# Experts: gated values turned one expert later, inside the next product; low weight parts shared three to three

## The chip, the cores and the metric

The kernel runs on one core of one Trainium2 chip. The metric is the device time of one execution in microseconds. The engines are named as in the profile: PE is TensorE (PEld its weight loads), ACT is ScalarE, DVE is VectorE, POOL is GpSimd, SP is SyncE, which here issues the weight loads. All matrices are float32; a product is made of three passes over a high and a low part (fp32r).

## The reference, cut to what matters

Two transformer blocks over 512 tokens of width 1024. The change lies in the last stage, a mixture of 16 experts in 4 groups of 4, each 1024 to 256 to 1024. Every token picks one group, and two experts in it:

```python
g_sel = argmax(hf @ w_r1 + b_r1)                 # one of 4 groups
top_p, top_i = top_k(softmax(e_logits[g_sel]), 2)   # two of its 4 experts
combine = one_hot(expert_id) * (g_w * top_p)     # zero for all other experts
hid = silu(hf @ w_gate[e]) * (hf @ w_up[e])      # 512 x 256 for each expert e
out = sum_e (combine[:, e] * hid) @ w_down[e]
x = x + out
```

## The kernel before, in words

**Order.** `make_order()` writes out one list of steps, and every engine runs through it in that order with its own part of each step. Semaphores of `Progress` (`X.after(key)` to wait, `X.done(key)` to signal) tie the engines together. Each engine works its own steps strictly one after the other.

**Sorted tokens.** `route 0` (DVE) finds the group of each token, `sort` its place in group order, `resort` (PE, ACT, DVE) turns the normalised tokens into `mix_hi`, `mix_lo`, sorted by group. The 512 sorted tokens are four blocks s of 128. A flag for each group and block says whether any token of the block is in the group. Visit v = 4e + s is expert e on block s. In this run's data 28 of the 64 visits are active: blocks 0 and 1 for experts 0 to 3, 1 and 2 for experts 4 to 7, 2 and 3 for 8 to 11, block 3 for 12 to 15. PE and DVE branch on the flag and do one tiny operation for a skipped visit (`skip`), which signals all of the visit's keys at once. ACT has no branch: it does its two activations for skipped visits too. `route 1` computes `combine`, and `combine_s` sorts it with PE.

**A visit, before.** On PE: 24 matmuls `ps[s] += mix * w` over 8 chunks k (left half of the 512 columns is gate, right half up); then `down(v - 4)`, the 12 matmuls of the same block's previous expert (not for the first expert of a group); then it waits for `hid` of this visit and transposes its two halves into bank 4. On ACT: `e_silu` = silu of the gate half after the up product, then `hid_hi` = rounded copy of the transposed values. On DVE: `hid` = up half times `e_silu`, then `hid_lo` = transposed values minus `hid_hi`, then `add(v - 4)`: two operations that add the down product, scaled by `combine_s`, to `y_exp`. `finish(v)` is the down product and `add` of a group's last expert; it stands ahead of the first visit of the next group on the same block. `hid` and `e_silu` have two slots, used in turn.

**Weights.** Each expert has six units of 128x1024: units 0 to 3 are gate and up (two chunks of k each), 4 and 5 are down. SP loads unit g into one of four slots `raw` once the low part of unit g - 4 is done. ACT makes the high part (line 1406), POOL (line 744) or DVE (line 2409) the low part `raw` minus high; `low_by(g)` says who: before, POOL for units 0 to 3, DVE for 4 and 5. Split parts lie in twelve slots, two experts deep: `w_hi`/`w_lo` and the first of `more_hi`/`more_lo` for even experts, the rest of `more`, `far_hi`/`far_lo`, `gap_w` and `end_w` for odd ones; a slot is free when PE is through with the expert two before. The steps `("weights", n)` in the order say up to which unit ACT, POOL and DVE split: at the end of expert e's visits units 4 and 5 of expert e + 1; ahead of visit (e + 1, 0) units 0, 1, 2 of expert e + 2; ahead of visit (e + 1, 1) unit 3 of expert e + 2. So between two experts ACT's queue holds the high parts of units 4, 5, 0, 1, 2, with unit 3 one visit later.

**Banks.** The up product of block s uses PSUM bank s, the transposes bank 4, down banks 5 and 6; `claim` waits for the last readers of a bank.

## Time and profile before

| | |
|---|---|
| time of three runs | 1829.16, 1830.31, 1831.88 us; median 1830.31 |
| profiled execution, its own time | 1819.03 us |
| its span, first to last instruction | 1817.2 us |
| mean granted clock of PE | 0.912 |
| PE busy | 1554.0 us, 86% |
| ACT, DVE, POOL busy | 686.0 (38%), 646.7 (36%), 565.4 us (31%) |
| memory traffic | 142.09 MB, mean 78 GB/s |
| expert stage, first visit to last down | 1455 to 1790 us |

The granted clock is the share of full speed that PE was given: 1.0 is 2.4 GHz, 0.5 is 1.2 GHz. Times in the timelines are counted from the span's start. A duration of a matmul in the profile overlaps the next one; the distance of two starts is what a matmul costs.

### The profile page before, as it was taken

What the parts mean: (1) busy time and instruction counts of PE and PEld (TensorE: products, weight loads), DVE (VectorE), ACT (ScalarE), POOL (GpSimd) and SP (SyncE); (2) the same over time, 40 slices, a digit from 0 to 9 for tenths busy, and PEclk for the clock granted to TensorE, in tenths of its full rate; (3) what the DMA queues carried; (4) which work ended last, traced back from release to release, by engine and by line L of the source; (5) the groups of instructions that cost most, each with busy time, mean ns of one, the idle gap of its engine ahead of it and who ended that gap; (6) DMA issues with size and microseconds to landing.
All of it is one profiled execution on the core that took longest, in us unless ns stands there. A gap on an engine that the chain in (4) does not pass through costs nothing. (4 is left out here: it accounts for less than half of the span.)

```text
span 1817.2 us, 18907 instructions
## 1 busy us (share of the span) xinstructions
PE 1554.0 (86%) x7008; PEld 1195.6 (66%) x7008; DVE 646.7 (36%) x1377; ACT 686.0 (38%) x1166; POOL 565.4 (31%) x253
## 2 busy tenths in 40 slices
PE   4998999989798899899557899989997688888877
PEld 3776666667576677767445687767875466666655
DVE  2276343233102322138844223043222443232333
ACT  4542224122445543243245424444232344343452
POOL 2264210003242233324200346522441444444460
PEclk9999998579899899999869999989998789998988
DMA  4222101002221122212100224411221144444451
GB/s 127 70 82 58 47 25 36 14 12 78 64 79 61 47 87 76 81 47 93 47 1 1 96 99 129 128 47 53 98 72 54 47 128 151 140 140 140 140 187 47
DMA packets 96000, 142.09 MB, mean 78 GB/s; under 512 B 11649, under 2 KB 46648, under 8 KB 95896
## 3 DMA queue, kind: packets, MB, share of 16 engines
q1 hardware_dynamic: 92948, 136.21, 23.4%
q10 hardware_dynamic: 2660, 4.45, 0.7%
q8 instruction: 69, 1.13, 0.3%
q14 instruction: 35, 0.29, 0.1%
q0 software_dynamic: 288, 0.02, 0.0%
HBM read 138.55 MB, written 2.10 MB: 77 GB/s over the span
## 5 line engine op out<-in xcount | busy, mean ns | idle before, releaser
L744 POOL TENSOR_TENSOR w_lo<-raw,w_hi 128x1024 fp32r<-128x1024 f32 (+1 forms) x191 | 455.7, 2404 | 1069.1 <-ACT w_hi L1406 1069.0
L1406 ACT ACTIVATE w_hi<-raw 128x1024 fp32r<-128x1024 f32 (+1 forms) x191 | 191.5, 1033 | 267.2 <-PE ps L796 241.6
L794 PE MATMUL ps<-w_hi,act_hi 128*128 128x512 f32 (+1 forms) x560 | 226.8, 405 | 17.9 <-ACT dq L1543 7.2
L795 PE MATMUL ps<-w_lo,act_hi 128*128 128x512 f32 (+1 forms) x560 | 222.0, 396 | 0.0
L796 PE MATMUL ps<-w_hi,act_lo 128*128 128x512 f32 (+1 forms) x560 | 221.5, 396 | 0.0
L794 PE MATMUL ps<-w_hi,mix_hi 128*128 128x512 f32 x432 | 174.1, 403 | 11.2 <-DVE mix_lo L1935 10.2
L795 PE MATMUL ps<-w_lo,mix_hi 128*128 128x512 f32 x432 | 172.1, 398 | 0.0
L796 PE MATMUL ps<-w_hi,mix_lo 128*128 128x512 f32 x432 | 171.9, 398 | 0.0
L794 PEld LDWEIGHTS ps<-w_hi,act_hi 128*128 128x128 f32 (+1 forms) x560 | 106.0, 189 | 49.1 <-POOL w_lo L744 8.3
L796 PEld LDWEIGHTS ps<-w_hi,act_lo 128*128 128x128 f32 (+1 forms) x560 | 105.8, 189 | 26.0
L794 PE MATMUL ps<-act_hi,w_hi 128*128 128x512 f32 (+5 forms) x288 | 110.0, 384 | 14.5 <-POOL w_lo L744 9.9
L795 PEld LDWEIGHTS ps<-w_lo,act_hi 128*128 128x128 f32 (+1 forms) x560 | 106.1, 189 | 23.1 <-issue 0.3
L795 PE MATMUL ps<-act_lo,w_hi 128*128 128x512 f32 (+5 forms) x288 | 109.9, 384 | 0.0
L796 PE MATMUL ps<-act_hi,w_lo 128*128 128x512 f32 (+5 forms) x288 | 108.4, 380 | 0.0
L794 PEld LDWEIGHTS ps<-w_hi,mix_hi 128*128 128x128 f32 x432 | 83.7, 194 | 31.2 <-DVE mix_lo L1935 9.4
L796 PEld LDWEIGHTS ps<-w_hi,mix_lo 128*128 128x128 f32 x432 | 83.5, 193 | 18.0
L795 PEld LDWEIGHTS ps<-w_lo,mix_hi 128*128 128x128 f32 x432 | 83.6, 193 | 17.2
L794 PEld LDWEIGHTS ps<-act_hi,w_hi 128*128 128x128 f32 (+3 forms) x288 | 53.7, 187 | 29.3 <-issue 6.4
L744 POOL TENSOR_TENSOR more_lo<-raw,more_hi 128x1024 fp32r<-128x1024 f32 x16 | 41.2, 2590 | 91.7 <-ACT more_hi L1406 91.7
L796 PEld LDWEIGHTS ps<-act_hi,w_lo 128*128 128x128 f32 (+3 forms) x288 | 53.9, 188 | 13.6 <-issue 2.1
L795 PEld LDWEIGHTS ps<-act_lo,w_hi 128*128 128x128 f32 (+3 forms) x288 | 53.6, 186 | 13.1 <-issue 1.6
L2386 DVE TENSOR_TENSOR hid<-ps,e_silu 128x256 f32<-128x256 f32 x28 | 11.9, 424 | 138.2 <-ACT e_silu L1575 138.2
(452 smaller groups left out, 2643.7 us busy)
## 6 DMA issues: line engine op xcount, KB each, us to landing
raw<-in_w_in SPq DMA_DIRECT2D x92, 512.0 KB, 3.4
raw<-in_w_gate SPq DMA_DIRECT2D x64, 256.0 KB, 3.0
raw<-in_w_up SPq DMA_DIRECT2D x64, 256.0 KB, 3.8
raw<-in_w_down SPq DMA_DIRECT2D x32, 512.0 KB, 4.5
raw<-in_w_out SPq DMA_DIRECT2D x16, 512.0 KB, 3.5
raw<-in_w_mem_kv SPq DMA_DIRECT2D x16, 512.0 KB, 3.8
raw<-in_w_o_gla SPq DMA_DIRECT2D x8, 512.0 KB, 3.4
raw<-in_w_o_dsa SPq DMA_DIRECT2D x8, 512.0 KB, 3.4
```

The lines of the kernel that those rows point to most:

```text
L744: pool.tensor_tensor(lo[:, 0:a], raw[:, g % RAW_SLOTS, 0:a], hi[:, 0:a].bitcast(F32), ALU.subtract).then_inc(*POOL.done(("w_lo", g)))
L794: pe.matmul(dst, l_hi, r_hi, start=start, stop=False, skip_group_check=skip)
L795: pe.matmul(dst, l_hi, r_lo, start=False, stop=False, skip_group_check=skip)
L796: return pe.matmul(dst, l_lo, r_hi, start=False, stop=stop, skip_group_check=skip)
L1406: nc.scalar.activation(split_slot(g)[0][:, 0:a], raw[:, g % RAW_SLOTS, 0:a], ACTF.Copy).then_inc(*ACT.done(("w_hi", g)))
L2386: dve.tensor_tensor(hid[:, v % 2, :], ps[:, s, D_EXP:2 * D_EXP], e_silu[:, v % 2, :], ALU.mult).then_inc(*DVE.done(("hid", v)))
```

## The change

- `hid` of visit v is no longer transposed at the end of visit v. The new `turn(v)` does it inside the up product of visit v + 4 (same block, next expert), ahead of chunk 4; ACT's `hid_high(v)` and DVE's `hid_low(v)` follow there. For the last expert of a group, `finish(v)` does turn, high and low parts and down.
- `finish` stands behind the visit of the same block instead of ahead of it.
- `hid` has one slot for each block (four), `e_silu` has one in all.
- `low_by`: POOL makes the low parts of units 0 to 2, DVE of 3 to 5. PE waits for unit 2's low part ahead of chunk 0 and for unit 3's ahead of chunk 6.
- `route 1` stands behind visit 3 instead of visit 0, next to `combine_s`.

```diff
--- before.py
+++ after.py
@@ -280,15 +280,13 @@
 
 
     for v in range(NT * N_EXP):
-        if v >= NT and v // NT % 4 == 0:
-            order += [("finish", v - NT)]
         if v % NT < 2:
             order += [("weights", E_UNITS * (v // NT + 1) + 3 + v % NT)]
         order += [("visit", v)]
-        if v == 0:
-            order += [("route", 1)]
+        if v >= NT and v // NT % 4 == 0:
+            order += [("finish", v - NT)]
         if v == NT - 1:
-            order += [("combine_s",)]
+            order += [("route", 1), ("combine_s",)]
         if v % NT == NT - 1:
             order += [("weights", E_UNITS * (v // NT + 2))]
     order += [("finish", NT * (N_EXP - 1) + s) for s in range(NT)]
@@ -468,8 +466,8 @@
         combine_s = sb("combine_s", [P, NT, N_EXP], SC + 59)
         so = sb("so", [P, 8, 16], SC + 59.25)
         flags = sb("flags", [P, 16], SC + 59.75, mybir.dt.int32)
-        hid = sb("hid", [P, 2, D_EXP], SC + 60)
-        e_silu = sb("e_silu", [P, 2, D_EXP], SC + 62)
+        hid = sb("hid", [P, NT, D_EXP], SC + 60)
+        e_silu = sb("e_silu", [P, D_EXP], SC + 56)
         skipped = sb("skipped", [1, 2, NT * N_EXP], SC + 72)
         iota = sb("iota", [P, SEQ], SC + 48)
         before_t = sb("before_t", [P, P], SC + 50)
@@ -594,7 +592,7 @@
 
         def low_by(g):
 
-            return DVE if g >= expert_unit and (g - expert_unit) % E_UNITS >= 4 else POOL
+            return DVE if g >= expert_unit and (g - expert_unit) % E_UNITS >= 3 else POOL
 
         def slot_free(g):
 
@@ -1238,6 +1236,15 @@
                 mm.then_inc(*done)
                 return done
 
+            def turn(v):
+
+                s = v % NT
+                pe.wait_ge(*DVE.after("hid", v))
+                claim(4, (ACT, ("hid_hi", v)), (DVE, ("hid_lo", v)))
+                for c in range(2):
+                    tr = pe.transpose(ps[:, 4, P * c:P * c + P], hid[:, s, P * c:P * c + P], ident[:, :])
+                tr.then_inc(*PE.done(("turn", v)))
+
             def visit(v):
 
 
@@ -1245,29 +1252,29 @@
                 g0 = expert_unit + E_UNITS * e
                 bank = s
                 with pe.If_ne(flag(v), 0):
-                    pe.wait_ge(*POOL.after("w_lo", g0 + 3))
                     claim(bank, (ACT, ("e_silu", v)), (DVE, ("hid", v)))
                     for k in range(KC):
+                        if k == 4 and e % 4:
+                            turn(v - NT)
+                        if k in (0, 6):
+                            low = g0 + (2 if k == 0 else 3)
+                            pe.wait_ge(*low_by(low).after("w_lo", low))
                         wh, wl = [x[:, 512 * (k % 2):512 * (k % 2) + 512] for x in split_slot(g0 + k // 2)]
                         rows = slice(P * s, P * s + P)
                         mm = product(ps[:, bank, :], mix_hi[:, k, rows], mix_lo[:, k, rows], wh, wl, k == 0, k == KC - 1)
-                    mm.then_inc(*PE.done(("up", v), *([("unit", g0 + i) for i in range(4)] if s == NT - 1 else [])))
+                    done = PE.done(("up", v), *([("unit", g0 + i) for i in range(4)] if s == NT - 1 else []))
+                    mm.then_inc(*done)
                     if e % 4:
-                        down(v - NT)
-                    pe.wait_ge(*DVE.after("hid", v))
-                    claim(4, (ACT, ("hid_hi", v)), (DVE, ("hid_lo", v)))
-                    for c in range(2):
-                        tr = pe.transpose(ps[:, 4, P * c:P * c + P], hid[:, v % 2, P * c:P * c + P], ident[:, :])
-                    done = PE.done(("turn", v))
-                    tr.then_inc(*done)
+                        done = down(v - NT)
                 with pe.Else():
-                    skip(done, 3 if e % 4 else 2)
+                    skip(done, 3 if e % 4 else 1)
 
             def finish(v):
                 with pe.If_ne(flag(v), 0):
+                    turn(v)
                     done = down(v)
                 with pe.Else():
-                    skip(done, 1)
+                    skip(done, 2)
 
             def unsort():
 
@@ -1566,20 +1573,28 @@
                     nc.scalar.activation(mix_hi[:, k, :], ps[:, k % 4, :], ACTF.Copy,
                                          scale=col("g_ffn_2", k)).then_inc(*ACT.done(("s_hi", k)))
 
-            def visit(v):
-
-                act.wait_ge(*PE.after("up", v))
-                if v >= 2:
-                    act.wait_ge(*ACT.after("e_silu", v - 2))
-                    act.wait_ge(*DVE.after("hid", v - 2))
-                nc.scalar.activation(e_silu[:, v % 2, :], ps[:, v % NT, 0:D_EXP], ACTF.Silu).then_inc(*ACT.done(("e_silu", v)))
+            last_turned = [None]
+
+            def hid_high(v):
+
                 act.wait_ge(*PE.after("turn", v))
-                if v:
-                    act.wait_ge(*DVE.after("hid_lo", v - 1))
+                if last_turned[0] is not None:
+                    act.wait_ge(*DVE.after("hid_lo", last_turned[0]))
                 if v >= NT:
                     act.wait_ge(*ACT.after("hid_hi", v - NT))
                     act.wait_ge(*PE.after("down", v - NT))
+                last_turned[0] = v
                 nc.scalar.activation(hid_hi[:, v % NT, :], ps[:, 4, 0:D_EXP], ACTF.Copy).then_inc(*ACT.done(("hid_hi", v)))
+
+            def visit(v):
+
+                if v // NT % 4:
+                    hid_high(v - NT)
+                act.wait_ge(*PE.after("up", v))
+                if v:
+                    act.wait_ge(*ACT.after("e_silu", v - 1))
+                    act.wait_ge(*DVE.after("hid", v - 1))
+                nc.scalar.activation(e_silu[:, :], ps[:, v % NT, 0:D_EXP], ACTF.Silu).then_inc(*ACT.done(("e_silu", v)))
 
             def unsort():
                 for s in range(NT):
@@ -1828,7 +1843,7 @@
                      "idx_scores": idx_scores, "dsa_prepare": dsa_prepare, "dsa_scale": dsa_scale, "dsa_scores": dsa_scores,
                      "dsa_turn": dsa_turn, "dsa_values": dsa_values, "mem_prepare": mem_prepare, "mem_scale": mem_scale,
                      "mem_scores": mem_scores, "mem_turn": mem_turn, "mem_values": mem_values, "route": route,
-                     "visit": visit, "unsort": unsort}
+                     "visit": visit, "finish": hid_high, "unsort": unsort}
             act.wait_ge(zeroed, 2)
             load_gains(act, 1)
             for step, *a in order:
@@ -2380,25 +2395,30 @@
             def visit(v):
                 e, s = divmod(v, NT)
                 with dve.If_ne(flag(v), 0):
+                    if e % 4:
+                        hid_low(v - NT)
                     dve.wait_ge(*ACT.after("e_silu", v))
-                    if v >= 2:
-                        dve.wait_ge(*PE.after("turn", v - 2))
-                    dve.tensor_tensor(hid[:, v % 2, :], ps[:, s, D_EXP:2 * D_EXP], e_silu[:, v % 2, :],
-                                      ALU.mult).then_inc(*DVE.done(("hid", v)))
-                    dve.wait_ge(*ACT.after("hid_hi", v))
-                    done = DVE.done(("hid_lo", v))
-                    dve.scalar_tensor_tensor(hid_lo[:, s, :], ps[:, 4, 0:D_EXP], 1.0, hid_hi[:, s, :].bitcast(F32),
-                                             ALU.mult, ALU.subtract).then_inc(*done)
+                    if v >= NT:
+                        dve.wait_ge(*PE.after("turn", v - NT))
+                    done = DVE.done(("hid", v))
+                    dve.tensor_tensor(hid[:, s, :], ps[:, s, D_EXP:2 * D_EXP], e_silu[:, :], ALU.mult).then_inc(*done)
                     if e % 4:
                         done = add(v - NT)
                 with dve.Else():
-                    skip(0, v, done, 3 if e % 4 else 2)
+                    skip(0, v, done, 3 if e % 4 else 1)
+
+            def hid_low(v):
+
+                dve.wait_ge(*ACT.after("hid_hi", v))
+                dve.scalar_tensor_tensor(hid_lo[:, v % NT, :], ps[:, 4, 0:D_EXP], 1.0, hid_hi[:, v % NT, :].bitcast(F32),
+                                         ALU.mult, ALU.subtract).then_inc(*DVE.done(("hid_lo", v)))
 
             def finish(v):
                 with dve.If_ne(flag(v), 0):
+                    hid_low(v)
                     done = add(v)
                 with dve.Else():
-                    skip(1, v, done, 1)
+                    skip(1, v, done, 2)
 
             def split_low(upto):
```

## Rows read from the trace of the kernel before

**Rows 1.** Busy time by stretch: expert stage; busy PE, PEld, DVE, ACT, POOL, clock, DMA.

```profile
1455.00:1790.00 335.00, 282.48 (x1194) 220.47 (x1194) 112.30 (x217) 135.30 (x226) 146.94 (x60) 0.91 0.44 139
```

**Rows 2.** Waits of PE from 1455 to 1792: total us, times, longest.

```profile
PE ps L1260 <- DVE hid L2386: 28.4, 15, 5.3
PE ps L794 <- DVE skipped L2366: 19.3, 7, 4.8
```

**Rows 3.** Timeline of PE, experts 2 and 3: start, length, what, wait before.

```profile
1503.53 0.50 PE L794 MATMUL ps<-w_hi,mix_hi 128*128 128x512 f32 x1
...
1513.60 0.44 PE L1260 MATMUL ps<-ident,hid 128*128 128x128 f32 x2 [1.60 <-DVE hid L2386]
1514.07 0.47 PE L794 MATMUL ps<-w_hi,mix_hi 128*128 128x512 f32 x1
...
1522.36 0.38 PE L1260 MATMUL ps<-ident,hid 128*128 128x128 f32 x2
...
1522.84 0.50 PE L794 MATMUL ps<-more_hi,mix_hi 128*128 128x512 f32 x1
```

**Rows 4.** Timeline of ACT and DVE in expert 2.

```profile
1506.04 3.90 ACT L1406 ACTIVATE more_hi<-raw 128x1024 fp32r<-128x1024 f32 x4
1507.12 2.36 DVE L2409 TENSOR_TENSOR more_lo<-raw,more_hi 128x1024 fp32r<-128x1024 f32 x2 [1.39 <-ACT more_hi L1406]
...
1511.76 1.06 ACT L1406 ACTIVATE far_hi<-raw 128x1024 fp32r<-128x1024 f32 x1 [1.83 <-DMA raw<-in_w_up]
...
1512.72 0.36 ACT L1575 ACTIVATE e_silu<-ps 128x256 f32<-128x256 f32 x1
```

**Rows 5.** Timeline in expert 10.

```profile
1681.16 0.24 PE L1222 MATMUL ps<-ones 128*1 128x1 f32 x4
...
1683.34 2.35 DVE L2409 TENSOR_TENSOR more_lo<-raw,more_hi 128x1024 fp32r<-128x1024 f32 x2
...
1688.11 1.06 ACT L1406 ACTIVATE far_hi<-raw 128x1024 fp32r<-128x1024 f32 x1 [2.67 <-DMA raw<-in_w_up]
...
1690.21 1.06 ACT L1406 ACTIVATE far_hi<-raw 128x1024 fp32r<-128x1024 f32 x1 [0.49 <-DMA raw<-in_w_up]
...
1692.60 0.44 PE L1260 MATMUL ps<-ident,hid 128*128 128x128 f32 x2 [2.82 <-DVE hid L2386]
```

**Rows 6.** Timeline where DVE and POOL work at once.

```profile
1472.89 2.34 POOL L744 TENSOR_TENSOR far_lo<-raw,far_hi 128x1024 fp32r<-128x1024 f32 x1 [8.52 <-ACT far_hi L1406]
1472.92 2.34 DVE L2307 TENSOR_TENSOR rt<-rt 128x16 f32<-128x16 f32 x1
...
1706.80 3.37 POOL L744 TENSOR_TENSOR w_lo<-raw,w_hi 128x1024 fp32r<-128x1024 f32 x1 [11.87 <-ACT w_hi L1406]
```

**Rows 7.** Timeline of PE: starts and ends of the groups of experts.

```profile
1541.74 0.38 PE L1260 MATMUL ps<-ident,hid 128*128 128x128 f32 x2
...
1569.60 0.47 PE L794 MATMUL ps<-more_hi,mix_hi 128*128 128x512 f32 x1
...
1631.64 0.38 PE L1260 MATMUL ps<-ident,hid 128*128 128x128 f32 x2
...
1661.95 0.47 PE L794 MATMUL ps<-more_hi,mix_hi 128*128 128x512 f32 x1
...
1724.02 0.38 PE L1260 MATMUL ps<-ident,hid 128*128 128x128 f32 x2
...
1771.93 0.79 PE L794 MATMUL ps<-more_hi,mix_hi 128*128 128x512 f32 x1 [0.65 <-POOL far_lo L744]
...
1784.71 0.47 PE L794 MATMUL ps<-gap_w,hid_hi 128*128 128x512 f32 x1 [2.40 <-DVE skipped L2366]
```

**Rows 8.** Timeline of DVE in the sort.

```profile
1429.57 2.25 DVE L2333 TENSOR_TENSOR so<-so 128x16 f32<-128x16 f32 x1
```

**Rows 9.** Busy time by stretch, behind two waits; columns as in rows 1.

```profile
1637.00:1642.20 5.20, 5.19 (x12) 3.82 (x12) 0.00 (x0) 2.75 (x5) 5.20 (x3) 0.52 0.90 283
1693.30:1697.30 4.00, 4.00 (x11) 3.20 (x12) 1.74 (x3) 0.15 (x1) 1.63 (x1) 0.59 0.74 233
```

## The prediction, made before the change ran

> **What bounds the kernel now.** I read the page first, then the busy time and clock of stretches, then what PE waited for, and last the timelines of single experts. The change touches the expert stage and a few steps ahead of it: 335 of 1817.2 us, in which PE is busy 282.5 us at a mean granted clock of 0.91 [rows 1]. So PE is the bound, and what can be had is its idle time and its time at 1.2 GHz. Its waits fall in two groups [rows 2]: 28.4 us ahead of the two transposes of `hid` (line 1260), and 19.3 us ahead of the down product (the "skipped" named there stands behind `add` on DVE, which frees banks 5 and 6); the latter come where the token group changes.
>
> Call T the start of the first active block's up product of an expert. From 1514.07 to 1522.36, 36 matmuls take 8.29 us: 0.230 each, so 5.5 for the up product and 2.8 for down [rows 3]. In expert 2, T is 1503.53 and the transposes start at T+10.1, having waited 1.6 [rows 3]. Why: `e_silu` stands on ACT behind the high parts of weight units 4, 5, 0, 1 and 2 (I call them the burst). ACT starts it at T+2.5; unit 2 can load only when DVE has done the low part of unit 4 (end T+4.8, half of the pair's 2.36), and ACT takes it up at T+8.2, 3.4 us later; ACT is free 0.96 after that, and from the start of `e_silu` to PE's start it is 0.88 (ACT's 0.36, the rest DVE's `hid` and latencies) [rows 3, 4]. In expert 10 the first active block is the third: T is 1681.4, behind the skips, unit 3 stands ahead of `e_silu` too and starts at T+8.8, and PE waits 2.8 us [rows 5]. The reader is to see that ACT's queue, not ACT's work, makes PE wait.
>
> **The change part by part.**
> *The transposes move into the next expert's up product.* The old values are long there, so PE's wait on `hid` goes. But `hid_hi` of the old block is now the first thing ACT does in a visit, behind the same burst, and PE needs it, and `hid_lo` after it, for the down product at T+5.5+0.44 = T+5.95 (0.44: the two transposes [rows 3]), where the transposes were due at T+8.3. The deadline comes 2.3 us earlier; the burst starts earlier only by the transposes and the `hid_hi` that left its front. Late next: `hid_lo`, with it down, then `add`.
>
> *Experts 2, 3 (blocks 0 and 1 active).* ACT still waits for DVE's skip behind `add`: burst at T+2.1 instead of T+2.5. Unit 2 is off ACT at 2.1+5.7+0.96 = T+8.7; `hid_hi` and `hid_lo` have the 128x256 shapes of `e_silu` and `hid`, so by the same 0.88 PE goes at T+9.55. PE stands 3.6 us. The expert lasts 9.55+2.75+8.7 (second visit with its transposes)+0.25 (skips) = 21.3, against 1522.84-1503.53 = 19.3 [rows 3]: for two experts **+4.1**.
>
> *Low part of unit 3 on DVE.* Where the first active block is not block 0, DVE meets it ahead of `hid_lo`. It lasts 1.2 us (two together 2.35 [rows 5]). And DVE and GpSimd do not run two-input work from SBUF side by side: a 128x16 sum on DVE lasted 2.34 us beside a GpSimd low part that started with it, and a GpSimd part that met a DVE one lasted 3.37 instead of 2.34 [rows 6]. For experts 5 to 7 I get, from T: burst 0.3, DVE's unit 4 done 2.6, unit 2 off ACT 7.05, block 0's empty pair 7.6, unit 3 taken up 2.6+1.1+4.5 = 8.2 (4.5 as in [rows 5]) and done 9.3. GpSimd has unit 0 from 3.3 and its three parts, one lengthened by DVE (2.7+2.34+2.34), last until 10.7; so DVE's unit 3 ends 11.9 and, with `hid_lo` close behind (0.4, the smaller half of the 0.88), PE goes at 12.3. Bound below: no holding, 11.0. I take the held one, since [rows 6] are these shapes. The expert is 12.3+2.75+8.7+0.35 = 24.1, three less the last skips 71.9, against 1631.64-1569.60 = 62.0 [rows 7]: **+9.9**. In experts 9 to 11 block 1's skip on DVE stands behind unit 3 and holds ACT's next `hid_hi` as well: burst -0.2, GpSimd until 10.65, DVE 11.8, skip 11.95, 0.88: PE goes at 12.9. Expert 24.65, three 73.7 against 1724.02-1661.95 = 62.1: **+11.6** [rows 7]. Experts 13 and 14 (one active block): GpSimd until 10.1, DVE 11.3, two empty ACT steps, PE at 12.9, expert 12.9+2.75+0.75 = 16.4.
>
> The Trainium skill (GPSIMD Engine Reference, Performance versus the Vector engine) puts elementwise work on VectorE at about twice GpSimd's speed. By that ratio alone the moved part costs the chain nothing: PE would go at about T+10.2 instead of 12.3 and 12.9 in eight experts, and the sum would be 20 us lower than mine. The ratio agrees with [rows 5, 6], 1.2 against 2.34; what the rows add is the place in DVE's queue.
>
> *Finish behind visit, at the three group changes.* The up product of the new group can cover the old group's DVE work. But down now needs `hid_hi`, which stands behind the whole burst: after group 0 (block 0's visit is skipped, so nothing covers it) the burst starts 2.25 us after the last down, unit 2 is off ACT at 8.9, an empty `e_silu` 0.3, 0.88: down starts at 10.1, a wait of some 9 us. Then down 2.75, up 5.5, one uncovered pair with the transposes 1.55, down 2.75, up 5.5, skips 0.5: 28.65 against 1569.60-1541.74 = 27.9 [rows 7]: **+0.8**. After group 1, unit 3 in front as above, down starts at 12.7: 31.2 against 1661.95-1631.64 = 30.3: **+0.9**; a wait of 4.8 [rows 2] makes room for one of 11. After group 2: 26.35, and with 2x16.4 for experts 13 and 14 it is 59.15 against 1771.93-1724.02 = 47.9: **+11.3** [rows 7].
>
> *The end.* Behind expert 15 no units 0 to 3 follow, so no stall: 8.7, and the last down starts 2.05 later (DVE's `add`, then `hid_lo`): 10.75 against 1784.71-1771.93 = 12.8 [rows 7]: **-2.0**.
>
> *Ahead of the experts.* GpSimd has three low parts instead of four beside the sort, so a DVE sum of 128x16, held for 2.25 us [rows 8], runs free: -2.1 on the path to the sorted tokens. Unit 3's low part on DVE then lies between sort and resort, hidden by PE's first resort products. `route 1` moves from visit 0 to visit 3 and starts 3.5 us later, behind visit 1's `hid`; its held sum [rows 6] goes (-2.2), and so do the waits of two transposes. Together **-1.9**, between -2.1 and +2.2.
>
> `e_silu` in one slot and `hid` in four cost nothing: each `e_silu` waits for a `hid` that was done while PE ran the product in between; without that cover, 0.4 a visit. PE's wait for unit 3 at chunk 6: nothing, that part is done an expert earlier.
>
> Sum at full clock: 4.1+9.9+11.6+0.8+0.9+11.3-2.0-1.9 = **+34.7**.
>
> *The clock.* In the 5.2 us behind a wait of 4.8, PE did the twelve matmuls of a down at a granted 0.52, that is at 1.2 GHz: 2.4 us lost; behind the 2.8 us wait of expert 10, 4 us at 0.59, 1.6 lost [rows 9]; behind the 1.6 us of expert 2 nothing [rows 3]. The lengths of before used above hold such losses, mine hold none. I add 1.7 for each of experts 2 and 3, and 2.0 (between 1.6 and 2.4) for each of eight longer stalls and three group changes: 3.4+22 = **+25**.
>
> Total +60. The profiled execution took 1819.0 us (span 1817.2, 1.8 around it); the median of the runs shown is 1830.3, 11 above, with nothing in the trace to say where. The sum is put on the median: 1890.
>
> **The rivals.**
> *Faster: the values are ready when down needs them.* Both waits of [rows 2] go (47.7), seven uncovered pairs in the finishes cost 1.0 each, the clock gives back half of the 0.09x335 = 30 us of [rows 1], and start and end help by 4: 1830-48+7-15-4 = 1770. It decides where ACT can take up unit 2 by T+4.0 in experts 2 and 3; the steps above say T+7.8. For it: PE's own waits are just those that the move removes. Against it: the burst's chain runs over three engines and a load, and the change shortens none. 8%.
> *Stalls as forecast, prices short.* GpSimd does not hold DVE in the burst (-13.6), and the clock costs between nothing and the 25: +21 to +46, 1851 to 1876. For it: the wait of 1.6 us brought no slow clock [rows 3]. 22%.
> *No change:* the burst starts so much earlier that it pays for the earlier deadline, 3 us an expert more than above. 3%.
> *Worse:* unit 2 lands 4.5 us behind the low part, as unit 3 does [rows 5], and each stall costs 2.4: +12+4, 1906 and above. 5%.
> The forecast, 1876 to 1906, has 62%.
>
> **How the numbers follow.** 1890 is the likeliest case. The range takes in short prices and forecast up to 1904: 1851 to 1904. Slower by over 0.2% (3.7 us, about what a measurement of this kernel can tell from no change): 62+22+5 = 89%; within it 3%; faster 8%.
>
> **What would show it.** PE's largest idle groups would be the first matmul of down (line 794, `gap_w` or `more_hi` with `hid_hi`) behind DVE's `hid_lo`: ten of 3.5 to 7 us and three of 9 to 11 or a little more; the waits of the transposes would be near zero. ACT's `hid_hi` of the first active block would start right behind unit 2 (or 3). GpSimd would have 45 low parts in the stage. Wrong if down follows the up product without a gap; half wrong if the gaps are 2 us shorter, or if DVE's unit 3 lasts 1.2 us each time; the clock part is wrong if the stretches behind the gaps show 1.0.

## The result, and the profile after

The changed kernel took 1889.47 us (median of four runs, 1887.75 to 1897.11). The kernel before took 1829.74 us (four runs, 1828.4 to 1831.88). The ratio is 1.0333, with a 95% interval of 1.0302 to 1.0365: 59.7 us slower. The prediction had said 1890 us, and had given 89% to slower.

The profiled execution took 1891.06 us (span 1889.2), against 1819.03 for the profiled one before. That is 72.0 us, 12 more than the medians are apart. The profiled execution before lay 11 us under its median, as the prediction said; what made it so fast I have not found. All lengths below are of this pair of profiles.

This is the busy time of the expert stage after, from the first up product to the end of the last down product. Its columns are those of [rows 1].

```profile
1457.40:1861.80 404.40, 284.94 (x1189) 224.28 (x1190) 138.03 (x231) 136.16 (x224) 109.59 (x45) 0.84 0.36 115
```

PE does the same work (282.5 us in [rows 1], 284.9 now), in 404 us instead of 335. The clock falls from 0.91 to 0.84. GpSimd has 45 low parts instead of 60.

What PE waited for, from 1455 to 1864 (total us, times, longest), to be held against [rows 2]:

```profile
PE ps L1245 <- ACT hid_hi L1587: 45.7, 9, 9.0
PE ps L1245 <- DVE skipped L2381: 37.9, 4, 11.6
PE ps L792 <- DVE hid_lo L2413: 24.4, 9, 7.5
PE ps L1196 <- DVE combine L2324: 10.4, 1, 10.4
```

Before, 47.7 us stood ahead of transposes and down products. Now it is 108.0 us, and most of it (83.6) stands ahead of the transposes (line 1245), which were to be free. Only 24.4 us stand where the prediction looked for all of it.

Expert 3 is of the kind that the forecast had right. The timeline of all engines, to be read with [rows 3, 4]:

```profile
1528.66 0.50 PE L792 MATMUL ps<-more_hi,mix_hi 128*128 128x512 f32 x1
...
1530.68 1.06 ACT L1413 ACTIVATE gap_w<-raw 128x1024 fp32r<-128x1024 f32 x1
1531.51 0.38 PE L1245 MATMUL ps<-ident,hid 128*128 128x128 f32 x2
...
1536.65 1.06 ACT L1413 ACTIVATE w_hi<-raw 128x1024 fp32r<-128x1024 f32 x1 [2.07 <-DMA raw<-in_w_up]
1537.61 0.37 ACT L1587 ACTIVATE hid_hi<-ps 128x256 fp32r<-128x256 f32 x1
...
1538.01 0.42 DVE L2413 SCALAR_TENSOR_TENSOR hid_lo<-ps,hid_hi 128x256 fp32r<-128x256 f32 x1 [3.87 <-ACT hid_hi L1587]
...
1538.54 0.47 PE L792 MATMUL ps<-more_hi,hid_hi 128*128 128x512 f32 x1 [3.90 <-DVE hid_lo L2413]
```

T, the start of the expert's first active up product, is 1528.66. The transposes run in mid-product, at T+2.9, without a wait. `hid_hi` could follow at once. But ACT is in its burst, and unit 2 lands late: ACT takes it up at T+8.0 and only then does `hid_hi`. PE starts down at T+9.9 after 3.90 us. The forecast was T+9.55 and 3.6.

Expert 10 is of the kind that the forecast had wrong. The same view, to be read with [rows 5]:

```profile
1716.05 0.50 PE L792 MATMUL ps<-w_hi,mix_hi 128*128 128x512 f32 x1
...
1717.31 2.35 DVE L2429 TENSOR_TENSOR more_lo<-raw,more_hi 128x1024 fp32r<-128x1024 f32 x2
...
1722.01 1.06 ACT L1413 ACTIVATE far_hi<-raw 128x1024 fp32r<-128x1024 f32 x1 [2.06 <-DMA raw<-in_w_up]
1722.97 0.37 ACT L1587 ACTIVATE hid_hi<-ps 128x256 fp32r<-128x256 f32 x1
...
1724.13 2.34 POOL L742 TENSOR_TENSOR far_lo<-raw,far_hi 128x1024 fp32r<-128x1024 f32 x1
1724.50 1.06 ACT L1413 ACTIVATE far_hi<-raw 128x1024 fp32r<-128x1024 f32 x1 [0.89 <-DMA raw<-in_w_up]
...
1725.59 1.97 DVE L2429 TENSOR_TENSOR far_lo<-raw,far_hi 128x1024 fp32r<-128x1024 f32 x1 [5.88 <-ACT far_hi L1413]
...
1727.48 0.13 DVE L2381 TENSOR_SCALAR skipped<-ones 1x1 f32<-1x1 f32 x1
1727.76 0.66 PE L1245 MATMUL ps<-ident,hid 128*128 128x128 f32 x2 [8.70 <-DVE skipped L2381]
```

Here blocks 0 and 1 are skipped and blocks 2 and 3 active. PE stops at T+3.0, in the middle of its up product, and stands 8.70 us. `turn(v)` calls `claim(4, ...)`: it may write bank 4 only when the readers of the turn before it have counted. That turn is the one of skipped block 1. Its reader on DVE is the skip at 1727.48, and this stands behind unit 3's low part, which stands behind unit 3's high part on ACT. So the transposes of an active block wait for a block that does nothing. The low part itself lasts 1.97 us instead of 1.22; GpSimd's began at 1724.13 and ended 1.09 us before it (more of this in the last section).

The groups' starts and ends after, to be held against [rows 7] (PE; the skips stand where a group's last expert ends):

```profile
1551.46 0.29 PE L1220 MATMUL ps<-ones 128*1 128x1 f32 x6
...
1582.33 0.50 PE L792 MATMUL ps<-more_hi,mix_hi 128*128 128x512 f32 x1
...
1654.81 0.34 PE L1220 MATMUL ps<-ones 128*1 128x1 f32 x8
...
1688.24 0.50 PE L792 MATMUL ps<-more_hi,mix_hi 128*128 128x512 f32 x1
...
1772.29 0.36 PE L1220 MATMUL ps<-ones 128*1 128x1 f32 x9
...
1784.24 0.66 PE L1245 MATMUL ps<-ident,hid 128*128 128x128 f32 x2 [11.56 <-DVE skipped L2381]
...
1842.99 0.50 PE L792 MATMUL ps<-more_hi,mix_hi 128*128 128x512 f32 x1
...
1857.35 0.76 PE L792 MATMUL ps<-gap_w,hid_hi 128*128 128x512 f32 x1 [0.98 <-DVE hid_lo L2413]
```

From these and [rows 7], in us:

| part | before | after | measured | forecast, clock included |
|---|---|---|---|---|
| experts 2 and 3 | 38.2 | 45.7 | +7.5 | +7.5 |
| change from group 0 to 1 | 27.9 | 30.9 | +3.0 | +2.8 |
| experts 5 to 7 | 62.0 | 72.5 | +10.4 | +15.9 |
| change from group 1 to 2 | 30.3 | 33.4 | +3.1 | +2.9 |
| experts 9 to 11 | 62.1 | 84.1 | +22.0 | +17.6 |
| change from 2 to 3, experts 13, 14 | 47.9 | 70.7 | +22.8 | +17.3 |
| expert 15 to the last down | 12.8 | 14.4 | +1.6 | -2.0 |
| norm and sort, to expert 2 | | | -1.2 | -1.9 |
| ahead of the experts, and behind them | | | +2.9 | 0 |
| sum | | | +72.1 | +60.1 |

The held sum of [rows 8] runs free, as forecast (DVE in the sort, after):

```profile
1433.05 0.18 DVE L2348 TENSOR_TENSOR so<-so 128x16 f32<-128x16 f32 x1
```

The stretches behind three waits and one without a wait in front, columns as in [rows 9]:

```profile
1538.50:1543.10 4.60, 4.56 (x13) 3.65 (x14) 0.27 (x1) 1.06 (x1) 2.50 (x2) 0.63 0.71 246
1727.70:1735.00 7.30, 7.24 (x27) 6.00 (x28) 0.85 (x2) 0.77 (x2) 0.00 (x0) 0.80 0.45 144
1784.20:1791.40 7.20, 6.18 (x15) 4.68 (x16) 0.45 (x2) 0.72 (x2) 0.00 (x0) 0.50 0.43 143
1595.60:1601.30 5.70, 5.70 (x26) 4.67 (x27) 1.83 (x3) 0.38 (x1) 0.00 (x0) 1.00 0.53 176
```

Behind 3.90 us of waiting the clock is 0.63, behind 11.56 us it is 0.50, which is 1.2 GHz; in the 7.3 us behind the 8.70 us of expert 10 it is 0.80. Twelve matmuls of a down then take up to 5.3 us instead of 2.8 (start to start: 1785.88 to 1791.13, against 1769.48 to 1772.29).

### The profile page after: what moved, and what is told of

It is laid out like the page before. It is cut to its first block and busy times, and to the rows that moved or that the text cites. A ratio compares the mean times of both kernels' runs of the same rounds, so it can differ in the third digit from the quotient of the medians.

```text
span 1889.2 us, 18908 instructions
## 1 busy us (share of the span) xinstructions
PE 1560.0 (83%) x7008; PEld 1201.8 (64%) x7008; DVE 672.5 (36%) x1393; ACT 687.4 (36%) x1166; POOL 525.3 (28%) x237
## 3 DMA queue, kind: packets, MB, share of 16 engines
q10 hardware_dynamic: 2660, 4.45, 0.8%
## 5 line engine op out<-in xcount | busy, mean ns | idle before, releaser
L742 POOL TENSOR_TENSOR w_lo<-raw,w_hi 128x1024 fp32r<-128x1024 f32 (+1 forms) x183 | 435.4, 2397 | 1123.8 <-ACT w_hi L1413 1123.8
L792 PE MATMUL ps<-w_hi,act_hi 128*128 128x512 f32 (+1 forms) x560 | 227.8, 407 | 19.5 <-POOL w_lo L742 8.1
L1245 PE MATMUL ps<-ident,hid 128*128 128x128 f32 x56 | 13.8, 336 | 83.6 <-ACT hid_hi L1587 45.7
L2390 DVE SCALAR_TENSOR_TENSOR y_exp<-ps,combine_s,y_exp 128x512 f32<-128x512 f32 x56 | 39.5, 746 | 76.2 <-PE ps L794 76.2
L1597 ACT ACTIVATE e_silu<-ps 128x256 f32<-128x256 f32 x64 | 24.3, 380 | 111.4 <-PE ps L794 109.0
```

Source lines behind the costliest of these rows:

```text
L742: pool.tensor_tensor(lo[:, 0:a], raw[:, g % RAW_SLOTS, 0:a], hi[:, 0:a].bitcast(F32), ALU.subtract).then_inc(*POOL.done(("w_lo", g)))
L792: pe.matmul(dst, l_hi, r_hi, start=start, stop=False, skip_group_check=skip)
L1245: tr = pe.transpose(ps[:, 4, P * c:P * c + P], hid[:, s, P * c:P * c + P], ident[:, :])
L1597: nc.scalar.activation(e_silu[:, :], ps[:, v % NT, 0:D_EXP], ACTF.Silu).then_inc(*ACT.done(("e_silu", v)))
L2390: op = dve.scalar_tensor_tensor(y, ps[:, 5 + n, :], combine_s[:, s, e:e + 1], y, ALU.mult, ALU.add)
```

## The experiments

Each kernel is timed against the kernel before on the same chip. The stage is the time in the profiled execution from the start of the first up product to the start of the last down product. It leaves out what varies ahead of the experts (last section), so parts are compared by it. But each stage length comes from a single execution: what it says of the difference to the kernel before and what the medians say lie 0.2 to 10.7 us apart in the rows below. A stage difference of a few us is therefore a hint and no proof. Medians decide on faster or slower.

| run | built on | ratio to before (95%) | median us | stage us |
|---|---|---|---|---|
| kernel before | | 1 | 1826.0 to 1829.7 | 329.5 |
| changed kernel | | 1.0333 (1.0302 to 1.0365) | 1889.47 | 399.9 |
| two banks | changed | 1.0313 (1.0278 to 1.0349) | 1887.16 | 391.1 |
| unit 3 on GpSimd | changed | 1.0286 (1.0242 to 1.0331) | 1879.46 | 383.3 |
| finish first | changed | 1.0328 (1.0285 to 1.037) | 1886.15 | 396.2 |
| split behind | changed | 1.0233 (1.0203 to 1.0262) | 1869.44 | 369.2 |
| unit 3 on VectorE | before | 1.0135 (1.0097 to 1.0173) | 1852.65 | 364.6 |
| delay alone | before | 1.0272 (1.0231 to 1.0313) | 1878.41 | 378.1 |
| spread, with delay | changed | 1.0089 (1.0056 to 1.0121) | 1843.31 | 345.2 |
| spread, no delay | before | 1.003 (0.9998 to 1.0061) | 1832.46 | 341.6 |
| spread 2, with delay | changed | 1.0073 (1.0047 to 1.0098) | 1837.78 | 343.0 |
| spread 2, unit 2 on VectorE | changed | 1.0097 (1.007 to 1.0125) | 1842.29 | 347.9 |
| spread 2, no delay | before | 0.9981 (0.9961 to 1.0) | 1822.05 | 321.8 |
| mixed order, no delay | before | 0.9981 (0.9962 to 1.0001) | 1823.68 | 325.5 |

### Two banks for the delayed transposes

```diff
-                claim(4, (ACT, ("hid_hi", v)), (DVE, ("hid_lo", v)))
+                claim(7 if v % 2 else 4, (ACT, ("hid_hi", v)), (DVE, ("hid_lo", v)))
```

The two transposes and their readers take the same bank. PE's skip, which wrote bank 7, now writes the bank that its step stands for, and waits for that bank's readers first; PE stood 1.5 us at such a skip, once.

> The changed kernel with one edit: the delayed transposes of even blocks go to bank 4 of PSUM, those of odd blocks to bank 7. Theory: in the groups whose first block is a skipped one before the active ones, TensorE stands at the transposes (8.93, 8.70 and 8.71 us in experts 9 to 11, 11.56 at the change from group 2 to group 3) because it may not write bank 4 before ScalarE and VectorE have read what the block before left there, although that block was skipped. With a second bank the transposes go ahead of the four last chunks, those four (about 4.2 us) then run beside the split, and the down product waits for what is left. Each of the five waits of experts 9 to 11, 13 and 14 that fall on the transposes, and the change 2 to 3, ends 3 to 4 us earlier: 12 to 20 us less than the changed kernel in all, 1870 to 1878 us; TensorE's idle time ahead of its transposes falls from 83.6 us to under 60. Rival: what is late is VectorE's own share (unit 3's low part, then the low part of the gated values), which stands behind the split whatever the bank: the down product then waits for as long as the transposes did, and the time is 1887 to 1892 us.

PE's waits in this run, from 1468 to 1863:

```profile
PE ps L792 <- DVE hid_lo L2420: 54.6, 12, 10.5
PE ps L1250 <- DVE skipped L2388: 20.8, 5, 8.6
PE ps L1250 <- ACT hid_hi L1594: 20.7, 4, 7.4
```

The wait at the transposes halves, from 83.6 to 41.5 us, but most of it comes back at the down product, where 24.4 us become 54.6. Expert 10 takes 23.8 us instead of 27.4, as the theory said, and expert 11 with the change to group 3 loses 6.9 together. But experts 13 and 14 keep 20 us each: their active block 3 needs bank 7, and the block that held it last is the skipped block 1, whose skip stands behind unit 3's low part. Experts 5 to 7 become dearer (25.3 to 27.3 us each, from 23.7 to 24.8). There the transposes now come early, the four chunks behind them run while ACT is still in its burst, and PE then stands 6.5 to 7.2 us at the down product. The stage loses 8.9 us of the 12 to 20 expected. By medians the gain can't be told from nothing, and the time, 1887.16 us, is the rival's. So the bank is shown as a cause of where PE waits, and of 3.6 us in expert 10; as a price of the whole, 9 us of stage are a hint. The rest is the queue behind it.

### Unit 3's low part back on GpSimd

```diff
-            return DVE if g >= expert_unit and (g - expert_unit) % E_UNITS >= 3 else POOL
+            return DVE if g >= expert_unit and (g - expert_unit) % E_UNITS >= 4 else POOL
```

> The changed kernel with one edit: the low part of the experts' unit 3 goes back from VectorE to GpSimd, as in the kernel before. Theory (VectorE's share stands ahead of the values that TensorE waits for): in experts 9 to 11, 13 and 14 the wait at the transposes loses what VectorE spends on that part, 1.97 us plus what it waits for a collision with GpSimd's, so about 2 us each, and as much at the two changes behind group 1: 10 to 14 us less than the changed kernel, 1875 to 1880 us. Experts 2, 3 and 5 to 7 stay within 1 us of 22.9 and 24.0. Rival (the wait is set by the units' high parts on ScalarE or by their transfers; VectorE's part lies in its shadow): no change, 1887 to 1892 us.

1879.46 us: inside the expected range. The wait of expert 9 falls from 8.93 to 6.67 us. What PE waits for ahead of the transposes is now always ACT (from 1463 to 1851):

```profile
PE ps L1245 <- ACT hid_hi L1587: 72.7, 13, 9.9
PE ps L792 <- DVE hid_lo L2413: 22.5, 9, 7.6
```

### Finish first

```diff
+        if v >= NT and v // NT % 4 == 0:
+            order += [("finish", v - NT)]
         if v % NT < 2:
             order += [("weights", E_UNITS * (v // NT + 1) + 3 + v % NT)]
         order += [("visit", v)]
-        if v >= NT and v // NT % 4 == 0:
-            order += [("finish", v - NT)]
```

> The changed kernel with one edit in the written order: at the change from one group of experts to the next, the finish of a block stands ahead of the split of the units and of the visit again, as in the kernel before. Theory (behind the visit, the finish's high and low part stand behind unit 2's or unit 3's split on ScalarE and VectorE): the stalls of 9.34, 11.61 and 11.56 us at the three changes shrink by 3 to 6 us each, 9 to 18 us less than the changed kernel, 1872 to 1881 us. Rival (the product of the visit covers the finish's chain of transposes, high part and low part; with the finish first nothing does): each active block's chain of about 2.1 us lies bare three times, and the time is 1889 to 1896 us.

The theory fell short: the stage loses 3.7 us and the median 3.3, not 9 to 18, and the intervals of this and the changed kernel overlap almost wholly. The change from group 0 to 1 gets 3.0 us shorter (27.8 instead of 30.9), the second stays as it was (33.5), the third loses 1.6. With the finish first, `hid_hi` stands ahead of unit 2 (PE waits 3.5 us instead of 7.5 for the first down), but then the chain from the up product to the next down lies bare, as the rival said. The two nearly cancel; the rival's 1889 to 1896 us did not come either.

### Split behind the visit

```diff
-        if v % NT < 2:
-            order += [("weights", E_UNITS * (v // NT + 1) + 3 + v % NT)]
         order += [("visit", v)]
...
+        if v % NT < 2:
+            order += [("weights", E_UNITS * (v // NT + 1) + 3 + v % NT)]
```

> The changed kernel with one edit in the written order: the split of the next expert's units 2 and 3 is queued behind the visit of block 0 and 1 and no longer ahead of it. Theory (each stall is the block's high and low part queued behind a split whose unit comes late): the 3.8 and 3.9 us waits of experts 2 and 3 and some 1.7 us at the experts before them go (about 9 us), those of experts 5 to 7 lose about 4 us each (12 us), experts 9 to 11 lose the wait on the skipped block but keep the split of unit 3 ahead of their own block (3 us each, 9 us), experts 13 and 14 keep theirs. 20 to 30 us less than the changed kernel, 1859 to 1870 us. Rival (the weights are what is late: the slots come free and the units land too late, and the split is needed where it stands): the next expert's first product waits for units 2 and 3 instead, by about as much as was saved, and the time is 1883 to 1895 us.

The stage lasts 369.2 us, 30.7 less than in the changed kernel; the time is 1869.44 us, inside the expected range. This is the clearest proof of the queue. Expert 3, all engines:

```profile
1533.66 1.06 ACT L1413 ACTIVATE gap_w<-raw 128x1024 fp32r<-128x1024 f32 x1
1534.61 1.06 ACT L1413 ACTIVATE end_w<-raw 128x1024 fp32r<-128x1024 f32 x1
...
1535.56 0.38 ACT L1587 ACTIVATE hid_hi<-ps 128x256 fp32r<-128x256 f32 x1
...
1537.07 2.00 ACT L1413 ACTIVATE w_hi<-raw 128x1024 fp32r<-128x1024 f32 x2
...
1537.55 0.47 PE L792 MATMUL ps<-more_hi,hid_hi 128*128 128x512 f32 x1 [0.80 <-DVE hid_lo L2413]
```

Only units 4 and 5 stand in front of `hid_hi`, and the late unit 2 stands behind it. The wait falls from 3.90 to 0.80 us, and expert 2 from 22.9 to 18.6. Expert 6 falls from 23.9 to 19.9 and expert 10 from 27.4 to 23.6, though there units split behind a skipped block still stand in front. Experts 13 and 14 stay at 19.0 and 20.3.

### Unit 3's low part on VectorE, alone

```diff
-            return DVE if g >= expert_unit and (g - expert_unit) % E_UNITS >= 4 else POOL
+            return DVE if g >= expert_unit and (g - expert_unit) % E_UNITS >= 3 else POOL
```

PE waits for units 0 to 2 at the first chunk and for unit 3 at the seventh, as in the changed kernel.

> The kernel before with one part of the change alone: the low part of the experts' unit 3 is VectorE's and no longer GpSimd's (TensorE waits for units 0 to 2 at the first chunk and for unit 3 at the seventh). Theory (VectorE's share stands ahead of the gated product in its queue, and GpSimd and VectorE hold each other): in experts 9 to 11, 13 and 14 the wait at the transposes grows by 1.2 to 2 us each, as much at two group changes, less 2 at the sort: 5 to 12 us more than the kernel before, 1835 to 1842 us. Rival (nothing stands behind VectorE's part while the values are turned in the same expert): within 3 us of the kernel before, 1827 to 1833 us.

1852.65 us, against 1826.04: 26.6 us, more than twice what the theory allowed and far from its rival. PE's waits ahead of the transposes are 28.1 us, as before (28.4); what grew is the wait ahead of down, from 19.3 us to this (from 1453 to 1822):

```profile
PE ps L794 <- DVE skipped L2368: 50.4, 11, 6.9
```

Expert 9, DVE, GpSimd and PE:

```profile
1675.74 2.33 POOL L744 TENSOR_TENSOR w_lo<-raw,w_hi 128x1024 fp32r<-128x1024 f32 x1
...
1676.43 2.73 DVE L2411 TENSOR_TENSOR w_lo<-raw,w_hi 128x1024 fp32r<-128x1024 f32 x1 [5.21 <-ACT w_hi L1408]
...
1679.08 0.13 DVE L2368 TENSOR_SCALAR skipped<-ones 1x1 f32<-1x1 f32 x1
...
1679.47 0.76 PE L794 MATMUL ps<-more_hi,hid_hi 128*128 128x512 f32 x1 [3.94 <-DVE skipped L2368]
```

I had looked only at the product `hid` behind this low part. The skip of block 1 stands behind it too. It is also the "reader" of banks 5 and 6, so PE's next down product waits for it: 3.94 us here, 6.88 and 6.87 in experts 10 and 11, where the kernel before did not wait at down. It is the same trap as the one at bank 4.

### The delay alone

The changed kernel with unit 3 on GpSimd, with the finish first and with `("route", 1)` behind visit 0.

> The changed kernel with unit 3's low part on GpSimd, the finish ahead of the split and of the visit, and the second half of the routing behind visit 0, all three as in the kernel before: what is left is the delay of the transposes by one expert, with the one slot for the activated values. Theory (the delay is the main price and the parts add up): the stage from the first up product to the last down product lasted 399.9 us in the changed kernel and 329.5 before; going back to GpSimd took 16.7 us of it and the finish 3.7, so some 380 us are left and the time is 1872 to 1880 us. Rival (the parts multiply: without VectorE's share in front the delayed values come in time for down): the stage lasts under 355 us, and the time is under 1856 us.

1878.41 us, stage 378.1: as expected. The delay with its slots costs 52 us by itself. Alone the delay and the low part on VectorE cost 52 and 27 us; together, in the changed kernel, with the finish and the place of `route 1` as well, they cost 60. My reading is that both lengthen the same wait; it was not tested further.

### The splits spread over the visits

```diff
         order += [("visit", v)]
...
+        if v % NT < 2:
+            order += [("weights", E_UNITS * (v // NT + 1) + 1 + v % NT)]
         if v % NT == NT - 1:
             order += [("weights", E_UNITS * (v // NT + 2))]
```

The two steps ahead of the visits are gone, and PE waits for each unit at its own two chunks. First with the delay and the two banks:

> The changed kernel with the two banks of the earlier run and the splits spread over the visits, each behind the visit of its block: unit 0 of the next expert behind block 0, unit 1 behind block 1, units 2 to 5 behind block 3; TensorE waits for each unit at its own two chunks. Theory (nothing but the split that stands ahead of the delayed values costs time): experts 2 and 3 take 18.6 us, 5 to 7 about 19.5, 9 to 11 about 20, 13 and 14 about 12, the group changes lose 5 us each; the stage takes 320 to 335 us and the time is 1808 to 1830 us, at or below the kernel before. Rival (units 0 and 1 of the next expert are loaded only when units 2 and 3 have been split, so TensorE now waits for weights at the start of each expert or each unit): 2 to 4 us for each of 12 experts, 1835 to 1870 us.

And in the kernel before, with unit 3's low part on VectorE:

> The kernel before with the same spread of the splits, unit 3's low part on VectorE and TensorE's waits unit by unit; the transposes stay in their own expert. Theory A (the waits of 1.6 to 3.3 us at the transposes in the kernel before have the same cause, a late unit's split ahead of the activation): they shrink to the bare 0.9 us, the stage loses 10 to 20 us, 1810 to 1820 us, as low as the same spread with the delay. Theory B (only the delay needs the early deadline, and the kernel before is bound otherwise): 1826 to 1836 us, and the version with the delay is lower by 10 us or more.

With the delay: 1843.31 us and a stage of 345.2, so 55 us of the stage come back by order and banks together. It is still 0.9% above the kernel before, above the 1830 that I expected and inside the rival's range. Without the delay: 1832.46 us, 1.0030 with an interval that reaches to 1. Theory B's numbers for this kernel hold, but its other half does not: the version with the delay is 11 us slower by the medians (their stages are 3.7 us apart), not faster. With the delay, PE now waits 2.1 us for GpSimd's low part of unit 2 in experts 2 and 3, as the rival said, and 7.2 and 7.8 us at the group changes.

### Units 4 and 5 later, products in place

```diff
         if v % NT == NT - 1:
-            order += [("weights", E_UNITS * (v // NT + 2))]
+            order += [("weights", E_UNITS * (v // NT + 1) + 4)]
...
-                nc.scalar.activation(e_silu[:, :], ps[:, v % NT, 0:D_EXP], ACTF.Silu)
+                nc.scalar.activation(hid[:, v % NT, :], ps[:, v % NT, 0:D_EXP], ACTF.Silu)
```

> The spread version with the delay, with two further edits: units 4 and 5 of an expert are split behind its own block 0 (and behind the finish there) and no longer at the end of the expert before, so only units 2 and 3 are split between two experts; and the activated values are written to the block's own slot of the gated values and multiplied in place, so ScalarE no longer waits for VectorE's product of the block before. Theory (what is left of the price is split work ahead of the delayed values at the group changes, 7.2, 7.8 and 8.1 us of waiting, and the split's late start in the others): the changes lose 3 to 5 us each, experts 2, 3, 5 to 7 some 1.5 us each, the stage goes from 345 to 320 to 328 us and the time to 1815 to 1828 us. Rival (the splits are only moved from one place ahead of the values to another): the waits come back at block 0 of each expert, 1838 us or more.

Then with unit 2's low part on VectorE and unit 3's on GpSimd:

> The same with one more edit: unit 2's low part is VectorE's and unit 3's GpSimd's, so that TensorE's fifth chunk no longer waits for GpSimd (2.1 us in experts 2 and 3, 1 to 1.8 us in experts 5 to 7 of the spread version). Theory: 1 to 1.5 us less for each of five experts, 5 to 8 us less than without the edit, 1808 to 1822 us. Rival (VectorE's part now stands ahead of its additions and the low parts of the values): nothing, or up to 5 us more.

And both edits of order and engines in the kernel before, transposes in their own expert:

> The kernel before, transposes in their own expert, with the same order of splits and the same engines for the low parts as the run with unit 2 on VectorE. Theory A (with the split out of the way the delay saves TensorE the bare 0.9 us of every block, some 24 blocks): this version is 10 to 20 us slower than that one. Theory B (the delay saves nothing because hid's high and low parts come late all the same): equal within 4 us or faster.

The first is 1837.78 us, a miss: 15 to 28 us were expected and 5.5 came, and the stage lost 2.2 us instead of 17 to 25. The second is 1842.29 us: the rival holds, moving the low part gains nothing (4.5 us more). The third is 1822.05 us, 20 us less than its twin with the delay. Theory A had it 10 to 20 us more; theory B, equal or faster, holds.

The order of splits and the engines of the low parts are the same in the last two, the twins. They are not equal in all else: the one with the delay also has the two banks, the product in place, the finish behind the visit and `route 1` behind visit 3. So the 20 us are not the delay's alone by the medians. Their stages are 26.0 us apart, and 23.6 of these lie inside the experts, where neither finish nor `route 1` stands. With the delay experts 5 to 7 are 4.1 us longer, 9 to 11 12.5, 13 and 14 6.3 and 15 3.4, but experts 2 and 3 are 2.5 us shorter (37.7 against 40.3); the three group changes together are 0.8 longer, the stretch ahead of expert 2 1.6. In this order of splits the delay costs where skipped blocks stand ahead of the first active one, and not where block 0 is active. The two banks and the product in place, which came with it, were not tested apart from it. Expert 10 of the second run, with the delay (all engines), and then of the third, without it (PE), show why:

```profile
1683.37 0.50 PE L791 MATMUL ps<-w_hi,mix_hi 128*128 128x512 f32 x1
...
1689.87 1.06 ACT L1419 ACTIVATE more_hi<-raw 128x1024 fp32r<-128x1024 f32 x1 [3.89 <-DMA raw<-in_w_up]
...
1692.17 1.06 ACT L1419 ACTIVATE more_hi<-raw 128x1024 fp32r<-128x1024 f32 x1 [0.70 <-DMA raw<-in_w_up]
1693.14 0.37 ACT L1593 ACTIVATE hid_hi<-ps 128x256 fp32r<-128x256 f32 x1
...
1694.30 0.59 PE L791 MATMUL ps<-gap_w,hid_hi 128*128 128x512 f32 x1 [4.51 <-DVE hid L2409]
```

```profile
1691.31 0.47 PE L794 MATMUL ps<-gap_w,hid_hi 128*128 128x512 f32 x1 [0.83 <-DVE skipped L2368]
...
1694.22 0.44 PE L1262 MATMUL ps<-ident,hid 128*128 128x128 f32 x2
```

The expert starts at 1683.37 there and at 1683.30 here. With the delay, PE is through with its up product at T+6.4 and wants `hid_lo`; but `hid_hi` stands behind units 2 and 3, which ACT takes up as they land, at T+6.5 and T+8.8, and down starts at T+10.9. Without the delay, down starts at T+8.0 after 0.83 us, and ACT's next work for PE is wanted only at the transposes behind down, at T+10.9, where PE does not wait for it. The expert takes 23.9 us with the delay and 20.2 without.

### The mixed order

> The kernel before, transposes in their own expert, with the spread order of the run before it only behind the visits of experts 4 to 10, where that run's experts were shorter (5 to 7 and 9 to 11: 18.8 to 20.2 us, against 19.3 to 22.2 in the kernel before); behind the other visits the order of the kernel before, since experts 1 to 3 had become 1 us longer each (TensorE waits 2.1 us for unit 2's low part) and the change from group 2 to 3 3.4 us longer (7.8 us of waiting instead of 4.6). Unit 2's low part is VectorE's where the order is the spread one, otherwise all as in the kernel before. Theory (the parts add up): the gain of the run before it, 4.6 us, and these 5 to 6 us on top: 1814 to 1820 us, 0.4 to 0.7% under the kernel before. Rival (what one expert gains, the next loses, since units arrive in one order through four slots): 1821 to 1827 us.

1823.68 us: the rival holds. Experts 2 and 3, which had become longer, are no longer so (19.5 and 19.4 us), but expert 11, the first behind the spread order, now waits 4.45 us at its transposes. What one place gains, the next gives back. Both versions without the delay lie 0.2% under the kernel before, with intervals that end at 1. I take neither for a proven gain.

## Why the prediction was right, and where it was right for the wrong reason

- **The bound.** "ACT's queue, not ACT's work, makes PE wait" held, and taking late units out from in front of `hid_hi` gave back 31 us of stage (split behind), or 55 together with the two banks (spread).
- **The earlier deadline.** The step "The deadline comes 2.3 us earlier" is the best reading of what remained when the order of splits and the engines were equal: 20 us between the medians of the twins, with the differences that are named there. It did not cost in experts 2 and 3, where the twin with the delay is 2.5 us shorter.
- **Experts 2 and 3.** Wait 3.8 and 3.9 us (3.6 forecast), and the down behind it took 1.6 us longer (4.4 instead of 2.8), where the clock term had 1.7. The sum is exact.
- **Group changes 0 to 1 and 1 to 2.** +3.0 and +3.1, forecast +2.8 and +2.9. The places of the waits differ (7.8 us stood at the transposes at the second change), the lengths do not.
- **Experts 5 to 7: too dear by 5.5 us.** The down started at T+12.4 in expert 6 (forecast 12.3). But PE had waited at the transposes, and the slow clock behind that wait fell on the four chunks that ran while DVE finished (4.25 us instead of 2.8, and the down behind them 2.8). The 2.0 us of clock that the forecast added for each did not come on top.
- **Experts 9 to 11, 13 and 14, and the third change: too cheap by 10 us.** The step that failed is "The old values are long there, so PE's wait on `hid` goes", taken to mean that the transposes need not wait at all. The forecast had the skip of block 1 on DVE behind unit 3's low part and let it hold ACT's next `hid_hi`. It did not see that `claim(4, ...)` makes PE wait for that same skip ahead of the transposes, with four chunks still to run behind it: the down started at T+16.0 in expert 10 instead of T+12.9. Two banks gave 3.6 us of this back in expert 10. In experts 13 and 14 the same claim holds PE for ACT's `hid_hi` of a skipped block, 7.85 and 9.03 us. The Trainium skill (PSUM — Partial Sum Buffer, PSUM bank collisions raise a hardware error) says that two engines must not touch one bank at the same time, reads included. By that rule the claim can't just be dropped; no run here shows a collision, they only moved the claim to another bank.
- **The end: 3.6 us too cheap.** The transposes of experts 14 and 15, the latter in the finish, waited 1.7 and 2.1 us for ACT's `hid_hi` of a skipped block, through the same claim, which the forecast left out.
- **Low part held by GpSimd.** 1.97 us in expert 10, and 2.73 in the run with the part alone, against 1.22 free. Going back to GpSimd gave 10 us of median and 16.7 of stage. The Trainium skill (GPSIMD Engine Reference, Performance versus the Vector engine) gives VectorE about twice GpSimd's speed, and the rows agree (1.22 against 2.34 us); by that rule alone the move costs the chain nothing, and the run with the part alone shows +26.6 us.
- **"What would show it" was half wrong.** The waits at the transposes were to be near zero; they are 83.6 us, and the down product has 24.4 us in nine waits, none over 7.5, where thirteen of 3.5 to 11 were to stand. The count of 45 low parts was right.

So the total was right partly by luck. The forecast missed the profiled pair by 12 us, with errors of 5.5 us one way and 14 us the other, and this pair is 12 us further apart than the medians, for a reason that no run shows. The mechanism was right in kind, and its second half (the bank) was missing.

## What to carry to other kernels

Moving a consumer later helps only if its producers' place in their queues moves too. Write down, for each wait that you add, the first thing in front of the producer that depends on a late transfer. A skipped branch still holds whatever its counters stand for: look at which bank or buffer the next active step claims, and in which queue the skip's signal stands. Before giving an engine more work because it is idle and faster, list who waits for the next instruction in its queue.

## What the runs showed of the hardware that I had not expected

The same instructions ahead of the experts took 7 to 14 us more in some profiled executions than in others: the stage before them ended at 1392 to 1396 us in some and at 1400 to 1407 in others. The difference starts in one stretch. Here is the kernel before, then the run with unit 3 on GpSimd, then the run "spread 2, no delay" (columns as in [rows 1]):

```profile
350.00:400.00 50.00, 49.74 (x228) 35.06 (x226) 15.81 (x47) 9.27 (x24) 2.38 (x1) 0.71 0.05 17
```

```profile
350.00:400.00 50.00, 49.96 (x185) 35.07 (x183) 12.68 (x38) 7.60 (x20) 2.38 (x1) 0.53 0.05 17
```

```profile
350.00:400.00 50.00, 50.00 (x180) 35.04 (x178) 13.10 (x38) 7.11 (x19) 2.36 (x1) 0.51 0.02 7
```

PE is busy all the time in each, with 228 matmuls at a granted 0.71 or 180 to 185 at 0.51 to 0.53, that is at 1.2 GHz. The 50 us ahead of it have 0.55 to 0.57 in all three. Of the fourteen profiled executions seven have 0.70 to 0.72 in this stretch and start the expert stage at 1453.5 to 1458.3 us; the other seven have 0.50 to 0.53 and start it at 1461.8 to 1468.1. What decides when the clock comes back stays open. It is why parts were compared by the stage and not by the whole profiled time. It may be a part of why the profiled execution before lay 11 us under its median, but it does not explain the 12 us of the pair: the profiled execution after had 0.71 in this stretch too, and lay 1.6 us above its median.

GpSimd and VectorE slow each other by more than one part's length: a low part on VectorE lasted 2.73 us beside GpSimd's instead of 1.22. The rows say more: it ended 1.09 us behind GpSimd's (1679.16 against 1678.07 in expert 9 of the run with unit 3 on VectorE), and so did all eleven lengthened low parts in the changed kernel's stage, of 1.8 to 2.7 us, each 1.07 to 1.09 us behind the end of GpSimd's. That is nearly the whole 1.22 us of a free one: VectorE's part makes hardly any way until GpSimd's has ended. The Trainium skill (GPSIMD Engine Reference, Specifications) names contention between the two for instructions with two inputs from SBUF; the trace agrees, and these numbers give its size.
